# Moving both halves of the activations in one matmul, and adding the bank's halves afterwards

## The chip, the core and the metric

The kernel runs on one core of a Trainium2 chip. TensorE multiplies, with a queue of its own for the loads of its stationary operand (PEld in the profile); VectorE (DVE) and ScalarE (ACT) do everything that is not a matmul, GpSimd (POOL) almost nothing, and SyncE (SP) issues the DMAs. The metric is the device time of one launch in microseconds: 2150.61 before, the median of three runs (2150.57 to 2150.96).

## What is computed

256 tokens of width 2048 go through three layers, in fp32 from end to end, with matmul results that have to be close to true fp32:

```python
h  = mamba2(x)            # x @ a_w_in -> z, B, C, x (conv of 4 taps, silu), dt; chunked scan; @ a_w_out
x  = layernorm(ALPHA * x + h)
h  = window_attention(x)  # @ kv_w, @ b_w_in (queries and gates), softmax in a window, @ b_w_out
x  = layernorm(ALPHA * x + h)
x  = x + neighbourhood_attention(rms_norm(x))   # @ na_w_qkv_2, @ na_w_o_2
x  = x + (relu(rms_norm(x) @ mlp_w1_2) ** 2) @ mlp_w2_2
```

The batch is 1, so the weights are read once, for 256 tokens.

## The kernel before, in words

**Units.** The weights come as 357 units of 1 MB each, in one fixed order (`plan()`). A unit is loaded into one of three `raw` buffers, split by ACT into a high part `whi` (rounded to the matmul's narrower format, fp32r) and by DVE into the rest, `wlo = raw - whi`, and used by 24 or 48 matmuls. The activations stand split in the same way, as `A1h`, `A1l` (16 tiles of 128 features x 256 tokens each) or `A2h`, `A2l`. A product is three products: high x high, low x high, high x low.

**Two forms.** 232 units are of form "B" (`token_block`): the activations are stationary, the weights move 512 columns at a time, and a PSUM bank holds 128 tokens x 512 features. 125 units are of form "A" (`feature_block`): the weights are stationary, 128 x 128 for each of the 16 tiles of the contraction, and the activations of all 256 tokens move, so the result stands features by tokens in half a bank:

```python
e.matmul(o, wh, A1h[:, k, :], start=k == 0, stop=False)
e.matmul(o, wh, A1l[:, k, :], start=False, stop=False)
last = e.matmul(o, wl, A1h[:, k, :], start=False, stop=k == KT - 1)
```

That is 16 x 3 = 48 matmuls of 256 columns in an A unit. Lines 872, 873 and 874 are these three, lines 889, 890 and 891 the three of form B.

**Which units are A.** In each of the 8 groups of the Mamba layer `B`, `C` and four `x` units (48 in all, their results go through the 4-tap convolution) and one `dt` unit in the first; 16 units `g` of attention gates; 60 units `up` of the MLP, in four runs of 12 or 16, the 16 with nothing between them on TensorE.

**Emptying a bank.** There are four main banks, and an A unit takes one of them. `late(u)` empties unit u's bank while unit u + 1 is on TensorE. For the convolution ACT makes the first tap from PSUM (`Identity` with scale and bias, line 1180), DVE adds the three others from PSUM (line 1525), and ACT applies silu in `post(u)` (line 1207). For `g` ACT copies (line 1188), for `up` ACT applies relu (line 1197), DVE squares (line 1596), ACT rounds (line 1211) and DVE subtracts (line 1607).

**Order on the engines.** One list of steps (`script()`) is walked by every engine, and each issues its own part of each step, so every engine's order is fixed. At the start of unit u comes `late(u-1)`, then the splits of unit u + 2 (`hi`, line 1163 on ACT; `lo`, line 1563 on DVE, which waits for `hi`), then `post(u-1)`, the matmuls, the load of unit u + 5, and last the side work that a timetable puts behind the unit (the steps of the scan, `ssd(g, n)`; the attention's, `att(j, n)`). On TensorE side work is small matmuls and transposes in four other banks; among them are lines 951 and 953 (`heads_out`) of the scan, which wait for a product of DVE (line 1754) that waits for an exponential of ACT (line 1286).

Of the kernel before, what the change touches and what calls it, by code (L numbers as in the profile page):

```python
# [7 lines left out]
P = 128  # L8
D = 2048
T = 256  # L10
NT = T // P
KT = D // P
# [61 lines left out]

W_CUM, W_E = 0, 2048
W_XDT, W_XD, W_ZS, W_Y = 5120, 6144, 7168, 8192
W_CBM, W_XF, W_DTS = 9216, 9600, 11136
# [229 lines left out]
def stack_kernel(nc, wst, xT, xtok, pos, cols, rows, nabias, consts, out):  # L307
# [6 lines left out]
    with ExitStack() as ctx:  # L314
# [93 lines left out]
        conv_a = Marks(sem("conv_a"), *[words("id silu")] * 48)  # L408
        conv_v = Marks(sem("conv_v"), *[words("j1 j2")] * 48)
# [203 lines left out]
        PT = [W[:, N_PT + i * 512:N_PT + (i + 1) * 512] for i in range(2)]  # L613
        hb = [W[:, M_HB + t * 512:M_HB + (t + 1) * 512] for t in range(NT)]
        cs_t, sn_t = (SM[:, c:c + 32].rearrange("p (t h f) -> p t h f", t=NT, h=2) for c in (S_COS, S_SIN))
        dt_rows = [W[0:NH_S, W_E + i * T:W_E + (i + 1) * T] for i in range(11)]

        def xr(t, c):
# [214 lines left out]
        def tensor_program(e):  # L833
# [14 lines left out]
            def unit(u, t, ks):  # L848
                form, tag, *_ = units[u]
                o = bank[BANK[u, t]]  # L850
                if 0 in ks and BEFORE.get((u, t)):
                    w.wait_ge(*emptied(*BEFORE[u, t]))
                if form == "A":
                    feature_block(u, o[:, 0:T])
                else:
                    token_block(u, t, o[:, :], ks)

# [274 lines left out]
        def scalar_program(e):  # L1132
            w = Spare(e)

            def begin():
                for k in range(4):
                    w.wait_ge(s_x0[k], 16)
                    e.activation(A1h[:, k, :], W[:, k * T:(k + 1) * T], ACT.Copy).then_inc(*x_a.inc(f"h{k}"))
                    piece_hi(0, k)
                for c in (1, 2, 3):  # L1140
                    w.wait_ge(s_x[c], 16)
                    h = A1h[:, 4 * c:4 * c + 4, :].rearrange("p k t -> p (k t)")
                    e.activation(h, W[:, c * 1024:(c + 1) * 1024], ACT.Copy).then_inc(*x_a.inc(f"c{c}"))
                    if c < 3:
                        for k in range(4):
                            piece_hi(c, k)
# [22 lines left out]
            def late(u):  # L1169
                form, tag, *_ = units[u]  # L1170
                kind = tag[0]
                if kind in ("B", "C", "x"):
                    n, slot, c0 = conv_of(tag)
                    g = tag[1]
                    w.wait_ge(*mm((u, 0)))
                    if g:
                        w.wait_ge(*ssd_p("cb" if slot < 2 else "px", g - 1))
                    w.wait_ge(s_co, 16)
                    x_staged()
                    e.activation(xf[slot], bank[BANK[u, 0]][:, 0:T], ACT.Identity, scale=CO[:, c0 + 3:c0 + 4],  # L1180
                                 bias=CO[:, c0 + 4:c0 + 5]).then_inc(*conv_a.inc("id", n))
                elif kind == "g":
                    j, i = tag[1:]
                    w.wait_ge(*mm((u, 0)))
# [3 lines left out]
                    e.activation(gs[j % 2][:, i, :], bank[BANK[u, 0]][:, 0:T], ACT.Copy).then_inc(*evac_a.inc((u, 0)))  # L1188
                    if i == 3:
                        w.wait_ge(*evac_a((u, 0)))  # L1190
                        e.activation(gs[j % 2], gs[j % 2], ACT.Silu).then_inc(*gs_a.inc("s", j))
                elif kind == "up":
                    i = tag[2]
                    w.wait_ge(*mm((u, 0)))
                    if ups.index(u) >= 4:
                        w.wait_ge(*up_v("sq", ups[ups.index(u) - 4]))
                    e.activation(W[:, M_R + i % 4 * T:M_R + (i % 4 + 1) * T], bank[BANK[u, 0]][:, 0:T],  # L1197
                                 ACT.Relu).then_inc(*evac_a.inc((u, 0)))
                elif form == "B" and closes(tag):
                    evac(u, 1)  # L1200

            def post(u):
                tag = units[u][1]
                if tag[0] in ("B", "C", "x"):
                    n, slot, _ = conv_of(tag)
                    w.wait_ge(*evac_v((u, 0)))
                    e.activation(xf[slot], xf[slot], ACT.Silu).then_inc(*conv_a.inc("silu", n))
# [313 lines left out]
        def vector_program(e):  # L1521
# [5 lines left out]
            def begin():  # L1527
# [6 lines left out]
                                    ALU.subtract).then_inc(*x_v.inc(f"h{k}"))  # L1534
                    piece_lo(0, k)
                for c in (1, 2, 3):
                    h, low = (a[:, 4 * c:4 * c + 4, :].rearrange("p k t -> p (k t)") for a in (A1h, A1l))
                    w.wait_ge(s_x[c], 16)
                    w.wait_ge(*x_a(f"c{c}"))
                    e.tensor_tensor(low, W[:, c * 1024:(c + 1) * 1024], h, ALU.subtract).then_inc(*x_v.inc(f"c{c}"))  # L1540
                    if c < 3:
                        for k in range(4):
                            piece_lo(c, k)
# [22 lines left out]
            def late(u):  # L1566
                form, tag, *_ = units[u]
                kind = tag[0]
                ps = bank[BANK[u, 0]] if form == "A" else None
                if kind in ("B", "C", "x"):  # L1570
                    n, slot, c0 = conv_of(tag)
                    w.wait_ge(*mm((u, 0)))
                    w.wait_ge(*conv_a("id", n))
                    for j in (1, 2, 3):
                        if j > 1:
                            w.wait_ge(*conv_v(f"j{j - 1}", n))
                        k = mul_add(xf[slot][:, j:], ps[:, 0:T - j], CO[:, c0 + 3 - j:c0 + 4 - j], xf[slot][:, j:],
                                    ALU.mult, ALU.add)
                        k.then_inc(*(conv_v.inc(f"j{j}", n) if j < 3 else evac_v.inc((u, 0))))
                elif kind == "dt":  # L1580
                    z, v, *_ = dt_rows
                    w.wait_ge(*mm((u, 0)))
                    w.wait_ge(*x_a("c3"))
                    w.wait_ge(*x_v("c3"))
                    w.wait_ge(s_co, 16)
                    e.tensor_scalar(z, ps[0:NH_S, 0:T], CO[0:NH_S, C_DTB:C_DTB + 1], None,
                                    ALU.add).then_inc(*evac_v.inc((u, 0)))
                    w.wait_ge(*evac_v((u, 0)))
                    mul_add(v, z, -1.0, z, ALU.mult, ALU.max).then_inc(*dt_v.inc("abs"))
                elif kind == "up":  # L1590
                    i = tag[2]
                    r = W[:, M_R + i % 4 * T:M_R + (i % 4 + 1) * T]
                    w.wait_ge(*evac_a((u, 0)))
# [4 lines left out]
                elif form == "B" and closes(tag):  # L1598
                    evac(u, 1)

            def post(u):
                tag = units[u][1]
# [747 lines left out]
```

## Time and profile before

| | |
|---|---|
| median of three runs | 2150.61 us |
| the profiled execution | 2151.69 us, of which the span of instructions is 2149.9 us |
| TensorE busy | 2140.8 us, 100% of the span |
| its weight loads | 1887.3 us, 88% |
| VectorE busy | 1345.8 us, 63% |
| ScalarE busy | 1066.0 us, 50% |
| granted clock of TensorE | full in all 40 slices of the page |
| DMA | 399.92 MB, 186 GB/s on the mean |

The three columns of an instruction group in the profile are busy time, the mean duration of one, and the idle time of its engine before it. Matmuls overlap in the array, so the duration of one (285 ns for 256 columns) is longer than the distance from one start to the next. That distance is what a matmul costs in a stream, and it is read from starts and counts.

### The profile page before, as it was taken

What the parts mean: (1) busy time and instruction counts of PE and PEld (TensorE: products, weight loads), DVE (VectorE), ACT (ScalarE), POOL (GpSimd) and SP (SyncE); (2) the same over time, 40 slices, a digit from 0 to 9 for tenths busy, and PEclk for the clock granted to TensorE, in tenths of its full rate; (3) what the DMA queues carried; (4) which work ended last, traced back from release to release, by engine and by line L of the source; (5) the groups of instructions that cost most, each with busy time, mean ns of one, the idle gap of its engine ahead of it and who ended that gap; (6) DMA issues with size and microseconds to landing.
All of it is one profiled execution on the core that took longest, in us unless ns stands there. A gap on an engine that the chain in (4) does not pass through costs nothing.

```text
span 2149.9 us, 31131 instructions
## 1 busy us (share of the span) xinstructions
PE 2140.8 (100%) x12836; PEld 1887.3 (88%) x12836; DVE 1345.8 (63%) x1766; ACT 1066.0 (50%) x1315; POOL 39.8 (2%) x28
## 2 busy tenths in 40 slices
PE   9999999999999999999999999999999999999999
PEld 8989889889897888888888888889889989988987
DVE  7777767767768867665675566555545445545543
ACT  6766565464554555663555545544334433433432
POOL 0000000000000000000010011000000000000000
PEclk9999999999999999999999999999999999999999
DMA  8554555554544744445564554455554555555553
GB/s 311 211 197 177 193 185 181 187 195 177 191 181 157 231 161 146 154 157 196 190 214 169 189 189 157 157 196 179 194 196 177 190 191 188 180 194 195 178 205 127
DMA packets 62715, 399.92 MB, mean 186 GB/s; under 512 B 7088, under 2 KB 9840, under 8 KB 16112
## 3 DMA queue, kind: packets, MB, share of 16 engines
q1 hardware_dynamic: 62576, 397.95, 51.9%
q8 instruction: 102, 1.67, 0.3%
q14 instruction: 37, 0.30, 0.0%
HBM read 395.75 MB, written 2.16 MB: 185 GB/s over the span
## 4 chain that ended last, share of the span: by engine, by line
PE 98%; DVE 1%; DMA 0%; issue 0%; SPq 0%; ACT 0%; POOL 0%; DVEq 0%
PE bank L889 20%; PE bank L891 19%; PE bank L890 19%; PE bank L872 11%; PE bank L873 11%; PE bank L874 11%; PE bank L951 1%; PE bank L1099 1%; PE bank L1035 1%; PE bank L1057 0%; PE bank L994 0%; PE bank L1087 0%; PE bank L964 0%; DMA raw<-wst 0%; PE bank L1112 0%; PE bank L1068 0%
## 5 line engine op out<-in xcount | busy, mean ns | idle before, releaser
L1563 DVE TENSOR_TENSOR wlo<-raw,whi 128x2048 fp32r<-128x2048 f32 x353 | 808.4, 2291 | 493.8 <-ACT whi L1163 438.1
L1163 ACT ACTIVATE whi<-raw 128x2048 fp32r<-128x2048 f32 x353 | 674.6, 1911 | 455.7 <-PE bank L891 450.4
L872 PE MATMUL bank<-A1h,whi 128*128 128x256 f32 x2000 | 569.2, 285 | 0.0
L874 PE MATMUL bank<-A1h,wlo 128*128 128x256 f32 x2000 | 566.7, 283 | 0.0
L873 PE MATMUL bank<-A1l,whi 128*128 128x256 f32 x2000 | 566.7, 283 | 0.0
L889 PE MATMUL bank<-whi,A2h 128*128 128x512 f32 x1024 | 401.6, 392 | 0.0
L891 PE MATMUL bank<-wlo,A2h 128*128 128x512 f32 x1024 | 399.2, 390 | 0.0
L890 PE MATMUL bank<-whi,A2l 128*128 128x512 f32 x1024 | 399.0, 390 | 0.0
L872 PEld LDWEIGHTS bank<-A1h,whi 128*128 128x128 f32 x2000 | 384.2, 192 | 1.5 <-issue 1.2
L873 PEld LDWEIGHTS bank<-A1l,whi 128*128 128x128 f32 x2000 | 384.2, 192 | 0.3
L874 PEld LDWEIGHTS bank<-A1h,wlo 128*128 128x128 f32 x2000 | 384.1, 192 | 0.0
L889 PE MATMUL bank<-whi,A1h 128*128 128x512 f32 x832 | 330.7, 397 | 3.3 <-ACT whi L1153 2.5
L891 PE MATMUL bank<-wlo,A1h 128*128 128x512 f32 x832 | 324.6, 390 | 0.0
L890 PE MATMUL bank<-whi,A1l 128*128 128x512 f32 x832 | 324.5, 390 | 0.0
L891 PEld LDWEIGHTS bank<-wlo,A2h 128*128 128x128 f32 x1024 | 192.3, 188 | 40.3
L889 PEld LDWEIGHTS bank<-whi,A2h 128*128 128x128 f32 x1024 | 192.4, 188 | 39.3 <-issue 0.3
L890 PEld LDWEIGHTS bank<-whi,A2l 128*128 128x128 f32 x1024 | 192.5, 188 | 38.9
L889 PEld LDWEIGHTS bank<-whi,A1h 128*128 128x128 f32 x832 | 156.4, 188 | 38.7 <-issue 5.2
L891 PEld LDWEIGHTS bank<-wlo,A1h 128*128 128x128 f32 x832 | 156.2, 188 | 33.0
L890 PEld LDWEIGHTS bank<-whi,A1l 128*128 128x128 f32 x832 | 156.5, 188 | 30.2
L1197 ACT ACTIVATE W<-bank 128x256 f32<-128x256 f32 x60 | 23.0, 383 | 190.7 <-PE bank L874 190.7
L1525 DVE SCALAR_TENSOR_TENSOR W<-bank,CO,W 128x255 f32<-128x255 f32 x144 | 69.2, 481 | 51.4 <-ACT W L1180 48.0
(220 smaller groups left out, 1318.4 us busy)
## 6 DMA issues: line engine op xcount, KB each, us to landing
raw<-wst SPq DMA_DIRECT2D x353, 1024.0 KB, 4.8
W<-cum_scratch SPq DMA_DIRECT2D x8, 1024.0 KB, 6.9
W<-rows SPq DMA_DIRECT2D x21, 256.0 KB, 5.4
raw<-wst SPq DMA_DIRECT2D x16, 256.0 KB, 7.9
W<-nabias SPq DMA_DIRECT2D x16, 160.0 KB, 3.7
XR<-xtok SPq DMA_DIRECT2D x2, 1024.0 KB, 8.2
out<-XR SPq DMA_DIRECT2D x8, 256.0 KB, 2.3
W<-xT SPq DMA_DIRECT2D x3, 512.0 KB, 7.9
```

Of the source, the lines that this page charges most:

```text
L872: e.matmul(o, wh, A1h[:, k, :], start=k == 0, stop=False)
L873: e.matmul(o, wh, A1l[:, k, :], start=False, stop=False)
L874: last = e.matmul(o, wl, A1h[:, k, :], start=False, stop=k == KT - 1)
L889: e.matmul(o, h, wh, start=opens and k == 0, stop=False)
L890: e.matmul(o, low, wh, start=False, stop=False)
L891: last = e.matmul(o, h, wl, start=False, stop=closes(tag) and k == 3)
L951: e.matmul(o[c:c + 64, pr * T:(pr + 1) * T], x[0], E[:, h * 384:h * 384 + T], start=True, stop=False)
L1035: tr = e.transpose(o[:, i * P:(i + 1) * P], S8[:, h, i * P:(i + 1) * P], ident)
L1163: e.activation(whi[:, u % 3, :], raw[:, u % 3, :], ACT.Copy).then_inc(*hi.inc((u, 3)))
L1197: e.activation(W[:, M_R + i % 4 * T:M_R + (i % 4 + 1) * T], bank[BANK[u, 0]][:, 0:T], ACT.Relu).then_inc(*evac_a.inc((u, 0)))
L1525: return e.scalar_tensor_tensor(out=o, in0=a, scalar=s, in1=b, op0=op0, op1=op1)
L1563: e.tensor_tensor(wlo[:, u % 3, :], raw[:, u % 3, :], whi[:, u % 3, :], ALU.subtract).then_inc(*lo.inc((u, 3)))
```

## The change

`A1h` and `A1l` become the two halves of one tile `A1`, so that for each k the high and the low activations are 512 columns in a row. An A unit then takes a whole bank: `wh` moves both halves in one matmul of 512 columns, and `wl` moves the high half alone, into the bank's second half. The first half of the bank ends up with high x high, the second with low x high plus high x low. They are added when the bank is emptied: ACT copies the second half to SBUF, DVE adds the first half from PSUM to it, and the bank is free after the add. What ACT did before (scale and bias, relu) moves to DVE, behind the add. The core of the diff, first the tile and the matmuls:

```diff
-        A1h = sb("A1h", [P, KT, T], F32R)
-        A1l = sb("A1l", [P, KT, T], F32R)
+        A1 = sb("A1", [P, KT, 2, T], F32R)
+        A1h, A1l = A1[:, :, 0, :], A1[:, :, 1, :]
...
-        ON_ACT = ("z", "g", "nv", "nk", "nq", "upb", "up")
+        ON_ACT = ("z", "nv", "nk", "nq", "upb")
...
             def feature_block(u, o):
-                    e.matmul(o, wh, A1h[:, k, :], start=k == 0, stop=False)
-                    e.matmul(o, wh, A1l[:, k, :], start=False, stop=False)
-                    last = e.matmul(o, wl, A1h[:, k, :], start=False, stop=k == KT - 1)
+                    both = A1[:, k, :, :].rearrange("p h t -> p (h t)")
+                    if k < KT - 1:
+                        e.matmul(o[:, :], wh, both, start=k == 0, stop=False)
+                        e.matmul(o[:, T:2 * T], wl, A1h[:, k, :], start=False, stop=False)
+                    else:
+                        e.matmul(o[:, T:2 * T], wl, A1h[:, k, :], start=False, stop=False)
+                        last = e.matmul(o[:, :], wh, both, start=False, stop=True)
```

Emptying a unit of the convolution, on ScalarE (`rest` is the bank's second half; `g`, `up` and `dt` copy it likewise):

```diff
-                    e.activation(xf[slot], bank[BANK[u, 0]][:, 0:T], ACT.Identity, scale=CO[:, c0 + 3:c0 + 4],
-                                 bias=CO[:, c0 + 4:c0 + 5]).then_inc(*conv_a.inc("id", n))
+                    e.activation(xf[slot], rest, ACT.Copy).then_inc(*rest_a.inc(u))
```

The same on VectorE:

```diff
-                    w.wait_ge(*conv_a("id", n))
-                    for j in (1, 2, 3):
-                        k = mul_add(xf[slot][:, j:], ps[:, 0:T - j], CO[:, c0 + 3 - j:c0 + 4 - j], xf[slot][:, j:],
-                                    ALU.mult, ALU.add)
+                w.wait_ge(*rest_a(u))
+                    e.tensor_tensor(xu, ps, xf[slot], ALU.add).then_inc(*evac_v.inc((u, 0)))
+                    e.tensor_scalar(xf[slot], xu, CO[:, c0 + 3:c0 + 4], CO[:, c0 + 4:c0 + 5], ALU.mult,
+                                    ALU.add).then_inc(*conv_v.inc("j0", n))
+                    for j in (1, 2, 3):
+                        mul_add(xf[slot][:, j:], xu[:, 0:T - j], CO[:, c0 + 3 - j:c0 + 4 - j], xf[slot][:, j:],
+                                ALU.mult, ALU.add).then_inc(*conv_v.inc(f"j{j}", n))
```

On VectorE for the gates, then for the MLP:

```diff
+                    e.tensor_tensor(x, ps, x, ALU.add).then_inc(*evac_v.inc((u, 0)))
...
-                    e.tensor_tensor(W[:, M_H + i % 4 * T:M_H + (i % 4 + 1) * T], r, r,
-                                    ALU.mult).then_inc(*up_v.inc("sq", u))
+                    e.tensor_tensor(r, ps, r, ALU.add).then_inc(*evac_v.inc((u, 0)))
+                    mul_add(W[:, M_H + i % 4 * T:M_H + (i % 4 + 1) * T], r, 0.0, r, ALU.max,
+                            ALU.mult).then_inc(*up_v.inc("sq", u))
```

The silu over a gate's four units also moves, from `late` of the fourth to its `post`, behind the split of the next weights.

The order of TensorE's instructions at the end of the `dt` unit, the first A unit. Before, its last two tiles of the contraction:

```order
L872 MATMUL bank2<-A1h,whi 128x256
L873 MATMUL bank2<-A1l,whi 128x256
L874 MATMUL bank2<-A1h,wlo 128x256
L872 MATMUL bank2<-A1h,whi 128x256
L873 MATMUL bank2<-A1l,whi 128x256
L874 MATMUL bank2<-A1h,wlo 128x256
```

After:

```order
L877 MATMUL bank2<-A1,whi 128x512
L878 MATMUL bank2<-A1,wlo 128x256
L880 MATMUL bank2<-A1,wlo 128x256
L881 MATMUL bank2<-A1,whi 128x512
L896 MATMUL bank0<-whi,A1 128x512
```

Three matmuls of 256 columns for each tile have become one of 512 and one of 256; in the last tile the two stand in the other order, and a unit of form B follows.

VectorE, a unit of the convolution in group 0 (its bank is bank0), between two splits of weights. Before:

```order
L1525 SCALAR_TENSOR_TENSOR W<-bank0,CO,W 128x255
L1525 SCALAR_TENSOR_TENSOR W<-bank0,CO,W 128x254
L1525 SCALAR_TENSOR_TENSOR W<-bank0,CO,W 128x253
L1563 TENSOR_TENSOR wlo<-raw,whi 128x2048
```

After:

```order
L1609 TENSOR_TENSOR W<-bank0,W 128x256
L1612 TENSOR_SCALAR W<-W,CO 128x256
L1536 SCALAR_TENSOR_TENSOR W<-W,CO 128x255
L1536 SCALAR_TENSOR_TENSOR W<-W,CO 128x254
L1536 SCALAR_TENSOR_TENSOR W<-W,CO 128x253
L1575 TENSOR_TENSOR wlo<-raw,whi 128x2048
```

Two instructions more stand ahead of the split, and the three taps now read SBUF.

VectorE in a run of `up` units. Before:

```order
L1607 TENSOR_TENSOR A2l<-W,A2h 128x256
L1596 TENSOR_TENSOR W<-W 128x256
L1563 TENSOR_TENSOR wlo<-raw,whi 128x2048
```

After:

```order
L1625 TENSOR_TENSOR A2l<-W,A2h 128x256
L1599 TENSOR_TENSOR W<-bank2,W 128x256
L1536 SCALAR_TENSOR_TENSOR W<-W 128x256
L1575 TENSOR_TENSOR wlo<-raw,whi 128x2048
```

One instruction more, the add from the bank, and the square has become a max with zero times the value. SP's and POOL's orders are the same in both kernels.

## Rows read from the trace of the kernel before

**Rows 1.** The page: busy time, granted clock, and the chain that ended last.
```profile
PE 2140.8 (100%) x12836; PEld 1887.3 (88%) x12836; DVE 1345.8 (63%) x1766; ACT 1066.0 (50%) x1315; POOL 39.8 (2%) x28
...
PEclk9999999999999999999999999999999999999999
...
PE 98%; DVE 1%; DMA 0%; issue 0%; SPq 0%; ACT 0%; POOL 0%; DVEq 0%
```
**Rows 2.** Groups by line: count | busy us, mean ns | engine idle before, releaser.
```profile
L872 PE MATMUL bank<-A1h,whi 128*128 128x256 f32 x2000 | 569.2, 285 | 0.0
...
L872 PEld LDWEIGHTS bank<-A1h,whi 128*128 128x128 f32 x2000 | 384.2, 192 | 1.5 <-issue 1.2
```
**Rows 3.** Windows: us, then busy us (instructions) by engine, clock, DMA, GB/s.
```profile
1608.84:1700.99 92.15, 92.15 (x769) 92.14 (x768) 48.84 (x47) 39.26 (x46) 0.00 (x0) 1.00 0.52 183
1700.99:1788.06 87.07, 87.07 (x386) 72.13 (x385) 42.35 (x25) 31.23 (x18) 0.00 (x0) 1.00 0.53 193
```
**Rows 4.** Timeline of TensorE where 512 columns meet 256: start, us, instruction.
```profile
1608.62 0.39 PE L891 MATMUL bank<-wlo,A2h 128*128 128x512 f32 x1
1608.84 0.28 PE L872 MATMUL bank<-A1h,whi 128*128 128x256 f32 x1
...
1700.88 0.28 PE L874 MATMUL bank<-A1h,wlo 128*128 128x256 f32 x1
1700.99 0.40 PE L889 MATMUL bank<-whi,A2h 128*128 128x512 f32 x1
```
**Rows 5.** Groups by line and form: emptying banks and its nearest kin.
```profile
L1180 ACT ACTIVATE W<-bank,CO 128x256 f32<-128x256 f32 x48 | 27.0, 563 | 93.2 <-PE bank L874 93.2
L1525 DVE SCALAR_TENSOR_TENSOR W<-bank,CO,W 128x255 f32<-128x255 f32 x48 | 23.0, 480 | 48.0 <-ACT W L1180 48.0
L1197 ACT ACTIVATE W<-bank 128x256 f32<-128x256 f32 x60 | 23.0, 383 | 190.7 <-PE bank L874 190.7
L2168 DVE TENSOR_TENSOR A2l<-bank,A2h 128x256 fp32r<-128x256 f32 x16 | 6.7, 424 | 9.9 <-ACT A2h L1502 9.9
L2037 DVE TENSOR_SCALAR W<-W,SM 128x256 f32<-128x256 f32 x32 | 11.1, 348 | 0.0
```
**Rows 6.** Timeline of DVE in one convolution unit of group 4.
```profile
430.39 1.52 DVE L1525 SCALAR_TENSOR_TENSOR W<-bank,CO,W 128x255 f32<-128x255 f32 x3 [1.67 <-ACT W L1180]
432.19 2.29 DVE L1563 TENSOR_TENSOR wlo<-raw,whi 128x2048 fp32r<-128x2048 f32 x1 [0.28 <-ACT whi L1163]
```
**Rows 7.** Timeline of ACT and DVE in one `up` unit.
```profile
1620.56 0.38 ACT L1197 ACTIVATE W<-bank 128x256 f32<-128x256 f32 x1 [3.27 <-PE bank L874]
1620.97 0.43 DVE L1596 TENSOR_TENSOR W<-W 128x256 f32<-128x256 f32 x1 [1.27 <-ACT W L1197]
1622.83 2.29 DVE L1563 TENSOR_TENSOR wlo<-raw,whi 128x2048 fp32r<-128x2048 f32 x1 [1.43 <-ACT whi L1163]
```
**Rows 8.** Window: a convolution unit of group 0; columns as in rows 3.
```profile
42.80:48.50 5.70, 5.70 (x50) 5.70 (x49) 5.53 (x9) 2.79 (x3) 0.00 (x0) 1.00 0.61 207
```
**Rows 9.** Timeline: a split on DVE in group 0, and the start of its unit.
```profile
52.38 2.28 DVE L1563 TENSOR_TENSOR wlo<-raw,whi 128x2048 fp32r<-128x2048 f32 x1
...
60.63 0.37 PE L872 MATMUL bank<-A1h,whi 128*128 128x256 f32 x1
```
**Rows 10.** Timeline: the scan's chain beside an A unit, and who takes it up.
```profile
103.82 0.39 PE L953 MATMUL bank<-W 128*64 128x128 f32 x4
...
106.16 1.49 ACT L1286 ACTIVATE W<-W 128x1536 f32<-128x1536 f32 x1
...
107.68 1.76 DVE L1754 TENSOR_TENSOR W<-W 128x1536 f32<-128x1536 f32 x1 [4.13 <-ACT W L1286]
...
110.09 0.65 PE L951 MATMUL bank<-W 128*64 128x256 f32 x4
```
**Rows 11.** Timeline: the latest split of weights ahead of an A unit.
```profile
924.46 2.29 DVE L1563 TENSOR_TENSOR wlo<-raw,whi 128x2048 fp32r<-128x2048 f32 x1 [4.77 <-issue]
...
929.10 0.37 PE L872 MATMUL bank<-A1h,whi 128*128 128x256 f32 x1
```

More of the change, by code:

```diff
@@ L407, in stack_kernel @@
         set_v = Marks(sem("constants_set"), words("warm mh"))
-        conv_a = Marks(sem("conv_a"), *[words("id silu")] * 48)
-        conv_v = Marks(sem("conv_v"), *[words("j1 j2")] * 48)
+        rest_a = Marks(sem("second_half_out"), [u for u in range(NU) if units[u][0] == "A"])
+        conv_a = Marks(sem("conv_a"), *[words("silu")] * 48)
+        conv_v = Marks(sem("conv_v"), *[words("j0 j1 j2 j3")] * 48)
         dt_v = Marks(sem("dt_v"), words("abs s rec su s2 p0 c15 c13 c11 c9 c7 c5 c3 pf p2 dt dl dq dh dr ch cl dte copy"))
@@ L1171, in late @@
                 kind = tag[0]
[L1172 to L1177, printed above, removed]
+                if form == "B":
+                    if closes(tag):
+                        evac(u, 1)
+                    return
+                rest = bank[BANK[u, 0]][:, T:2 * T]
+                w.wait_ge(*mm((u, 0)))
+                if kind == "dt":
+                    x_staged()
                     w.wait_ge(s_co, 16)
-                    x_staged()
-                    e.activation(xf[slot], bank[BANK[u, 0]][:, 0:T], ACT.Identity, scale=CO[:, c0 + 3:c0 + 4],
-                                 bias=CO[:, c0 + 4:c0 + 5]).then_inc(*conv_a.inc("id", n))
+                    e.activation(dt_rows[0], rest[0:NH_S, :], ACT.Identity,
+                                 bias=CO[0:NH_S, C_DTB:C_DTB + 1]).then_inc(*rest_a.inc(u))
                 elif kind == "g":
                     j, i = tag[1:]
-                    w.wait_ge(*mm((u, 0)))
                     if j >= 2:
@@ L1187, in late @@
                         w.wait_ge(*gate_v((j - 2, 2, 1)))
[L1188 to L1191, printed above, removed]
+                    e.activation(gs[j % 2][:, i, :], rest, ACT.Copy).then_inc(*rest_a.inc(u))
                 elif kind == "up":
                     i = tag[2]
-                    w.wait_ge(*mm((u, 0)))
                     if ups.index(u) >= 4:
                         w.wait_ge(*up_v("sq", ups[ups.index(u) - 4]))
[L1197 to L1200, printed above, removed]
+                    e.activation(W[:, M_R + i % 4 * T:M_R + (i % 4 + 1) * T], rest, ACT.Copy).then_inc(*rest_a.inc(u))
+                else:
+                    n, slot, _ = conv_of(tag)
+                    g = tag[1]
+                    if g:
+                        w.wait_ge(*ssd_p("cb" if slot < 2 else "px", g - 1))
+                    x_staged()
+                    e.activation(xf[slot], rest, ACT.Copy).then_inc(*rest_a.inc(u))
             def post(u):
@@ L1205, in post @@
                     n, slot, _ = conv_of(tag)
+                    w.wait_ge(*conv_v("j3", n))
+                    e.activation(xf[slot], xf[slot], ACT.Silu).then_inc(*conv_a.inc("silu", n))
+                elif tag[0] == "g" and tag[2] == 3:
+                    j = tag[1]
                     w.wait_ge(*evac_v((u, 0)))
-                    e.activation(xf[slot], xf[slot], ACT.Silu).then_inc(*conv_a.inc("silu", n))
+                    e.activation(gs[j % 2], gs[j % 2], ACT.Silu).then_inc(*gs_a.inc("s", j))
                 elif tag[0] == "up":
@@ L1536, in begin @@
                 for c in (1, 2, 3):
[L1537 removed]
+                    h, low = (a[:, 4 * c:4 * c + 4, :] for a in (A1h, A1l))
+                    x = W[:, c * 1024:(c + 1) * 1024].rearrange("p (k t) -> p k t", k=4)
                     w.wait_ge(s_x[c], 16)
                     w.wait_ge(*x_a(f"c{c}"))
[L1540 removed]
+                    e.tensor_tensor(low, x, h, ALU.subtract).then_inc(*x_v.inc(f"c{c}"))
                     if c < 3:
@@ L1568, in late @@
                 kind = tag[0]
[L1569 to L1572, printed above, removed]
-                    w.wait_ge(*conv_a("id", n))
-                    for j in (1, 2, 3):
-                        if j > 1:
-                            w.wait_ge(*conv_v(f"j{j - 1}", n))
-                        k = mul_add(xf[slot][:, j:], ps[:, 0:T - j], CO[:, c0 + 3 - j:c0 + 4 - j], xf[slot][:, j:],
-                                    ALU.mult, ALU.add)
-                        k.then_inc(*(conv_v.inc(f"j{j}", n) if j < 3 else evac_v.inc((u, 0))))
-                elif kind == "dt":
-                    z, v, *_ = dt_rows
[L1582 to L1587, printed above, removed]
+                if form == "B":
+                    if closes(tag):
+                        evac(u, 1)
+                    return
+                ps = bank[BANK[u, 0]][:, 0:T]
+                w.wait_ge(*mm((u, 0)))
+                w.wait_ge(*rest_a(u))
+                if kind == "dt":
+                    z, v, *_ = dt_rows
+                    e.tensor_tensor(z, ps[0:NH_S, :], z, ALU.add).then_inc(*evac_v.inc((u, 0)))
                     w.wait_ge(*evac_v((u, 0)))
                     mul_add(v, z, -1.0, z, ALU.mult, ALU.max).then_inc(*dt_v.inc("abs"))
+                elif kind == "g":
+                    x = gs[tag[1] % 2][:, tag[2], :]
+                    e.tensor_tensor(x, ps, x, ALU.add).then_inc(*evac_v.inc((u, 0)))
                 elif kind == "up":
```

20 lines of the change are left out of this document (13 added, 7 removed).

## The prediction

> **What bounds the kernel now.** I read the page first. TensorE is busy in all of the span at the full clock, VectorE 63% and ScalarE 50% of it, and of the chain that ended last 98% is TensorE [rows 1]. So only what shortens TensorE's own stream, or makes it wait, can move the time; work on the other engines counts where it becomes late for TensorE.
>
> A busy TensorE says little of its pace, since matmuls overlap: one of 256 columns is recorded with 285 ns, and its weight load with 192 ns [rows 2]. The pace is read from starts and counts. The first window is a run of 16 `up` units with nothing between them: 16 x 48 = 768 matmuls of 256 columns (the 769th reaches in from before) in 92.15 us, or 119.99 ns each. The second is the run of 16 units of form B behind it: 384 matmuls of 512 columns in 87.07 us, or 226.74 ns each [rows 3]. The difference of the two, 106.75 ns, is what 256 more columns cost. Taken off either pace it leaves the same remainder: 119.99 - 106.75 = 13.24 ns, and 226.74 - 213.50 = 13.24 ns. It is paid once for each matmul with its load, however long the matmul is. The change moves as many columns as before (768 for each tile), in two matmuls in place of three.
>
> **The change part by part.**
>
> *Matmuls.* For each tile of an A unit: before 3 x 119.99 = 359.97 ns; after 226.74 + 119.99 = 346.73 ns; saved 13.24 ns. There are 2000 tiles (125 units of 16, the count of line 872 [rows 2]), so 26.5 us; a unit shrinks by 0.212 us, from 5.76 to 5.55. The trace has no stream in which 512 and 256 columns take turns, so the pair is bounded from both sides. Above, the pair could cost what three cost now, 360 ns, and nothing is gained. Below, the short matmul could cost its columns alone, 106.75 ns, for another 26.5 us; I exclude this, as the remainder stands whole at both lengths. I take the sum of the two paces because the trace shows both changes of length: from a 512 to the next start 0.22 us, and from a 256 to the start of a 512 0.11 us, each the ordinary distance of its own length [rows 4].
>
> The Trainium skill, "TensorE: Matmul & The Clock Gate", section "Back-to-back issue gap", gives N / 2.4 + 2.5 ns between starts at the warm clock, so a fixed part of only 2.5 ns. By it the three would cost 327.5 ns and the two 325.0 ns, the change would save 5.0 us, and the time would be 2145.6. The trace does not agree with it: 13.24 ns is left in both runs.
>
> *Emptying, ScalarE.* In the 48 convolution units a copy of 256 columns from PSUM (383 ns) takes the place of the scaled one (563 ns); in `up` and `g` a copy replaces an operation of its own size [rows 5]. ScalarE gets 8.6 us less, off the path.
>
> *Emptying, VectorE.* Each A unit gets an add with one side in PSUM; the nearest row has 424 ns. A convolution unit also gets a scale-and-bias in SBUF, 348 ns, while its three taps stay at 480 ns or a little under, now that they read SBUF [rows 5]. The square of `up` keeps its count. At most 48 x 0.77 + 76 x 0.42 = 69 us more on VectorE, 1415 of 2124 us, 67%. Is any of it in TensorE's way? By kind of unit:
>
> - Convolution, groups 1 to 7. The taps end at 431.91 and the split follows at 432.19, 0.28 us later, on ScalarE's account [rows 6]. The new chain starts 0.18 us earlier and is 0.77 us longer, so it ends at 432.50 and the split starts 0.3 us later. It is for the unit after next, which starts at about 441. Nothing.
> - Convolution, group 0, beside the small operations for `dt`. VectorE is busy 5.53 of 5.70 us there [rows 8], and the next three units look alike. With 0.77 more and a unit of 5.55 us it falls behind by some 0.75 us a unit, 3 us over four. The split of that stretch is done at 54.66 and its unit starts at 60.63, 5.97 us later [rows 9]. This cover holds, with about 3 us left; without it the rest would be a wait of TensorE, paid once.
> - `up`. VectorE's work ends at 1621.40 and it then waits 1.43 us for ScalarE's split [rows 7]. The add of 0.42 goes into this wait. The bank is free after about 1 us, and three more A units come before it is needed again.
> - `g`. Here too the add stands where VectorE waits for the split. The latest split ahead of an A unit is done at 926.75 and used at 929.10, 2.35 us later [rows 11]. It is far above the 0.21 us by which TensorE comes earlier.
> - The scan's chain. After line 953 ScalarE makes an exponential and VectorE a product that ends at 109.44, and TensorE takes it up at 110.09, behind an A unit: 0.65 us to spare [rows 10]. The unit between them shrinks by 0.21, which leaves 0.44. This is what is late next. ScalarE's silu now waits for a chain some 0.4 us longer, so the margin could go; I count 0.2 us for such small waits altogether.
>
> *Loads.* Weights are asked for at 1 MB in 5.55 us; form B's run already takes 1 MB in 5.44 us at a DMA share of 0.53 [rows 3]. No new bound.
>
> **Sum.** 26.5 - 0.2 = 26.3 us. The profiled execution took 2151.69 us, 1.79 outside the span, which gives 2125.4; the median of the runs is 1.08 lower, so **2124.3 us**.
>
> **The rivals.**
>
> 1. *The others' latency eats part of it.* In the `up` runs nothing but the splits stands beside TensorE, and their 60 x 0.212 = 12.7 us are safe. In the Mamba layer and the attention, 65 units, TensorE is followed closely by chains on the two other engines. If each took back what its unit saved, 13.8 us would go and the time would be 2138. For it: 0.65 us of margin [rows 10] and VectorE almost full in group 0 [rows 8]. Against it: the margins are several times 0.21 us elsewhere, and the chain of waits holds 1% of VectorE [rows 1]. Any time between 2129 and 2142 is this case: 0.06.
> 2. *The pair saves next to nothing,* because a short matmul between long ones costs more than in its own stream, or the fixed part is the 2.5 ns of the page named above: 2145 to 2151. Against it: the equal remainder [rows 3]. 0.04, half of it within 0.2%.
> 3. *Slower: the load of `wl` is no longer hidden.* Should the weight load of the short matmul begin only when the long one has left the array, the 192 ns of the load [rows 2] would stand in place of 120 ns: 72 ns more, 59 ns net of the saving, and 2000 pairs make 118 us, 2268 us. It decides from 13.24 ns a pair. Against it: in form B's run loads are hidden behind 512 columns, 72.13 us of loads in 87.07 with no loss [rows 3], and at a change of length too [rows 4]. 0.03.
>
> The forecast has 0.87, with a range of its own of 2122.5 to 2127: 13.24 ns is known to some tenths of a nanosecond (0.1 ns is 0.2 us), and small waits may cost up to 2 us or TensorE's present small waits shrink with the earlier start.
>
> **How the numbers follow.** The low end, 2121, is the forecast with 3 us more for a pair that is a little cheaper than the sum of its parts. The high end, 2130, takes in the first 6 us of rival 1. What is left out is the rest of rival 1, and rivals 2 and 3, together about 0.12. Faster by over 0.2% (4.3 us, about what a measurement of this kernel can tell from no change): the forecast, rival 1 and half of rival 2, 0.95. Within: the other half, 0.02. Slower: rival 3, 0.03.
>
> **What would show each step.** In the profile after, 16 `up` units of one run should take 16 x 16 x 0.34673 = 88.8 us in place of 92.15, and form B's run its 87.1 unchanged. TensorE should have 2000 matmuls and loads fewer and still be the whole chain. The split behind a convolution unit should start some 0.3 us later against its unit's start, with no idle time of TensorE released by VectorE or ScalarE. I am wrong if the pair in an `up` run is not 347 ns (then the matmul's cost was misread), or if it is and the Mamba layer shrinks by less than 10 us for its 49 units (then it is rival 1, and the group of waits names the chain).

## The result, and the profile after

The changed kernel takes **2137.63 us** (median of 4 runs, 2137.34 to 2138.11) where the kernel before took 2150.59 (4 runs, 2150.31 to 2150.96): a ratio of 0.994, 95% interval 0.9923 to 0.9957. It gains 13.0 us where 26.3 were forecast, and lies outside the range of 2121 to 2130. The profiled execution took 2137.87 us with a span of 2135.6.

The page of the changed kernel: the span, busy time by engine, the granted clock, the chain that ended last by engine, and groups of instructions (count | busy us, mean ns | idle before, releaser).

```profile
span 2135.6 us, 27302 instructions
...
PE 2126.5 (100%) x10836; PEld 1778.7 (83%) x10836; DVE 1413.4 (66%) x1938; ACT 1060.3 (50%) x1316; POOL 39.8 (2%) x28
...
PEclk9999999999999999999999999999999999999999
...
PE 94%; DVE 1%; ACT 0%; issue 0%; POOL 0%; DVEq 0%
...
L877 PE MATMUL bank<-A,whi 128*128 128x512 f32 x1875 | 668.8, 399 | 0.0
L878 PE MATMUL bank<-A,wlo 128*128 128x256 f32 x1875 | 526.4, 281 | 0.0
...
L1200 ACT ACTIVATE W<-bank 128x256 f32<-128x256 f32 x60 | 23.1, 386 | 184.5 <-PE bank L881 184.5
L1599 DVE TENSOR_TENSOR W<-bank,W 128x256 f32<-128x256 f32 x60 | 25.4, 424 | 72.4 <-ACT W L1200 72.4
```

TensorE has its 2000 matmuls and 2000 loads fewer and is 94% of the chain that ended last. That chain is TensorE's from 109.31 us on; before this it runs over VectorE and ScalarE, and it can be followed back only to 79.01 us (below, under the silus). The idle of lines 877 and 878 is 0.0, so within a unit there is no wait longer than what two matmuls overlap, and a loss there is one of pace (the emptying alone, below, has the same waits and no loss). The windows of the changed kernel over the same two stretches as in [rows 3] (a run of 16 `up` units, then form B's 16), and, third, the whole Mamba layer; columns as there:

```profile
1599.71:1690.16 90.45, 90.45 (x513) 78.43 (x512) 55.19 (x62) 39.28 (x46) 0.00 (x0) 1.00 0.52 186
1690.16:1777.21 87.05, 87.05 (x386) 72.08 (x384) 42.76 (x26) 31.23 (x18) 0.00 (x0) 1.00 0.54 193
...
25.07:688.14 663.07, 661.76 (x3519) 554.44 (x3517) 526.31 (x659) 376.67 (x449) 5.90 (x9) 1.00 0.54 194
```

Form B keeps its 87.05 us. The `up` run takes 90.45 us: 1.70 less than the 92.15 of before, and half of the 3.39 that were forecast (88.76). It holds 256 pairs, so a pair costs 353.3 ns and not 346.7, although VectorE, ScalarE and the loads leave nothing waiting. The timeline of TensorE inside one of its units shows where it goes:

```profile
1622.67 0.40 PE L877 MATMUL bank<-A,whi 128*128 128x512 f32 x1
1622.90 0.28 PE L878 MATMUL bank<-A,wlo 128*128 128x256 f32 x1
1623.02 0.40 PE L877 MATMUL bank<-A,whi 128*128 128x512 f32 x1
1623.26 0.28 PE L878 MATMUL bank<-A,wlo 128*128 128x256 f32 x1
1623.38 0.40 PE L877 MATMUL bank<-A,whi 128*128 128x512 f32 x1
1623.62 0.28 PE L878 MATMUL bank<-A,wlo 128*128 128x256 f32 x1
1623.73 0.40 PE L877 MATMUL bank<-A,whi 128*128 128x512 f32 x1
```

Three pairs take 1623.73 - 1622.67 = 1.06 us, 353 ns each. The next start comes 0.23 or 0.24 us behind a long matmul and 0.11 or 0.12 behind a short one. The trace's starts, to the nanosecond, repeat every three pairs (236 113 233 117 241 120):

```
233 113  233 117  241 120  236 113  233 117  241 120 ...   ns from one start to the next
```

So the long distances are 9.9 ns over the 226.74 of [rows 3] in the mean, and the short ones 3.3 ns under 119.99: 6.6 ns net a pair, or 106 ns a unit.

14 of the 125 units run otherwise. From their third pair on all of them hold a steady 230.0 and 116.6 ns, together 346.7: the forecast pair, although neither distance is that of its own run. This is one of them, in the Mamba layer of the same execution (three pairs in 1.04 us):

```profile
193.24 0.39 PE L877 MATMUL bank<-A,whi 128*128 128x512 f32 x1
193.47 0.28 PE L878 MATMUL bank<-A,wlo 128*128 128x256 f32 x1
193.58 0.39 PE L877 MATMUL bank<-A,whi 128*128 128x512 f32 x1
...
194.28 0.39 PE L877 MATMUL bank<-A,whi 128*128 128x512 f32 x1
```

**The account.** 111 units x 0.106 = 11.8 us. TensorE also waits twice at line 958 in the scan of group 0, 1.45 us in all (below). 26.5 - 11.8 - 1.45 = 13.3 us, and 13.0 were measured.

### The profile page after: what moved, and what is told of

Its sections match the earlier page's. It is cut to its first block, busy times and chain, and to the rows that moved or that the text cites. A ratio compares the mean times of both kernels' runs of the same rounds, so it can differ in the third digit from the quotient of the medians.

```text
span 2135.6 us, 27302 instructions
## 1 busy us (share of the span) xinstructions
PE 2126.5 (100%) x10836; PEld 1778.7 (83%) x10836; DVE 1413.4 (66%) x1938; ACT 1060.3 (50%) x1316; POOL 39.8 (2%) x28
## 4 chain that ended last, share of the span: by engine, by line
PE 94%; DVE 1%; ACT 0%; issue 0%; POOL 0%; DVEq 0%
PE bank L896 19%; PE bank L898 19%; PE bank L897 19%; PE bank L877 18%; PE bank L878 9%; PE bank L881 1%; PE bank L958 1%; PE bank L1106 1%; PE bank L880 1%; PE bank L1042 1%; PE bank L1064 0%; PE bank L1001 0%; PE bank L1094 0%; PE bank L971 0%; PE bank L1075 0%; PE bank L1119 0%
## 5 line engine op out<-in xcount | busy, mean ns | idle before, releaser
L877 PE MATMUL bank<-A,whi 128*128 128x512 f32 x1875 | 668.8, 399 | 0.0
L878 PE MATMUL bank<-A,wlo 128*128 128x256 f32 x1875 | 526.4, 281 | 0.0
L877 PEld LDWEIGHTS bank<-A,whi 128*128 128x128 f32 x1875 | 352.2, 188 | 81.8 <-issue 1.2
L878 PEld LDWEIGHTS bank<-A,wlo 128*128 128x128 f32 x1875 | 354.2, 189 | 4.5
L896 PE MATMUL bank<-whi,A 128*128 128x512 f32 x832 | 330.6, 397 | 2.2 <-ACT whi L1160 1.2
L898 PE MATMUL bank<-wlo,A 128*128 128x512 f32 x832 | 324.3, 390 | 0.0
L897 PE MATMUL bank<-whi,A 128*128 128x512 f32 x832 | 324.2, 390 | 0.0
L896 PEld LDWEIGHTS bank<-whi,A 128*128 128x128 f32 x832 | 156.3, 188 | 37.8 <-issue 5.8
L898 PEld LDWEIGHTS bank<-wlo,A 128*128 128x128 f32 x832 | 156.2, 188 | 33.2
L897 PEld LDWEIGHTS bank<-whi,A 128*128 128x128 f32 x832 | 156.6, 188 | 30.4
L1536 DVE SCALAR_TENSOR_TENSOR W<-W,CO 128x255 f32<-128x255 f32 x144 | 69.5, 483 | 5.1
L2210 POOL TENSOR_TENSOR SM<-SM 128x2 f32<-128x2 f32 (+2 forms) x24 | 39.6, 1654 | 1399.0 <-DVE SM L1789 649.2
```

The costliest lines, as they stand in the source:

```text
L877: e.matmul(o[:, :], wh, both, start=k == 0, stop=False)
L878: e.matmul(o[:, T:2 * T], wl, A1h[:, k, :], start=False, stop=False)
L896: e.matmul(o, h, wh, start=opens and k == 0, stop=False)
L897: e.matmul(o, low, wh, start=False, stop=False)
L898: last = e.matmul(o, h, wl, start=False, stop=closes(tag) and k == 3)
L1536: return e.scalar_tensor_tensor(out=o, in0=a, scalar=s, in1=b, op0=op0, op1=op1)
```

## The experiments

The theories, by the numbers that the expectations use: (1) a change of a matmul's length costs, whichever way the rest is arranged (1a: a fixed price for each change); (2) a long matmul of an A unit is dear whatever stands beside it; (3) the longer emptying makes TensorE wait, at line 958 above all; (4) the short matmul is dear, or makes the next one late, because it goes into the bank's second half; (5) it is the interleaved layout of the high and low activations. Each experiment leaves the rest of the changed kernel as it is; diffs are against it.

**Long ones first.** All 16 long matmuls of a unit, then its 16 short ones: the same work with one change of length each way.

```
-                    if k < KT - 1:
-                        e.matmul(o[:, :], wh, both, start=k == 0, stop=False)
-                        e.matmul(o[:, T:2 * T], wl, A1h[:, k, :], start=False, stop=False)
-                    else:
-                        e.matmul(o[:, T:2 * T], wl, A1h[:, k, :], start=False, stop=False)
-                        last = e.matmul(o[:, :], wh, both, start=False, stop=True)
+                    e.matmul(o[:, :], wh, both, start=k == 0, stop=False)
+                for k in range(KT):
+                    wl = wlo[:, s, k * P:(k + 1) * P]
+                    last = e.matmul(o[:, T:2 * T], wl, A1h[:, k, :], start=False, stop=k == KT - 1)
```

> The changed kernel, but each A unit issues its 16 matmuls of 512 columns first and then its 16 of 256, so the two lengths take turns once in a unit in place of 16 times. Theory 1 (taking turns costs it: in the changed kernel the pair takes 353.1 ns, 236.5 + 116.6, where 346.7 was forecast): the long ones return to 227 ns and the short ones to 120, an A unit takes 5.55 us in place of 5.65, and the time is 2137.6 - 12.7 = 2125 us. Theory 2 (512 moving columns of activations cost 236 ns whatever stands beside them, in this form of unit): the long ones stay at 236, the short ones go to 120, and the time is 2137 to 2144 us.

Measured: 2129.55 us (2128.91 to 2131.16) beside 2150.80, ratio 0.990 (0.9885 to 0.9915), 8.1 us under the changed kernel. Its `up` run, as a window:

```profile
1597.09:1686.13 89.04, 89.04 (x514) 78.72 (x512) 55.19 (x62) 39.26 (x46) 0.00 (x0) 1.00 0.54 189
```

A unit is 5.567 us, 20 ns over 16 x 346.7. Its distances show that the loss sits at the change and dies out behind it:

```
233 236 229 232 231 227 226 227 ... 226 | 114 119 120 120 ... 120
```

After the change to 512 five starts are late by 6, 9, 2, 5 and 4 ns, 26 together; after the change back two are early, 7 together. 26 - 7 is the 19 or 20 ns of a unit.

The 2125 us of theory 1 were missed by 4.6. The 20 ns that are left in a unit make 2.5 us over 125 units. The waits in front of the scan's matmuls (line 956 here) rose from 1.3 to 2.6 us of idle time. And in the profiled execution, itself 1.6 us above the median, TensorE waits for VectorE's split of the weights in group 0, which it does not do in the changed kernel:

```profile
65.65 3.91 PE L876 MATMUL bank<-A,whi 128*128 128x512 f32 x16 [1.18 <-DVE wlo L1573]
```

**Four products.** All matmuls long, so that the low weights meet the low activations too: a product that the reference's arithmetic leaves out, and 256 more columns a tile. There is no change of length at all inside a run. In place of the six lines that the first diff removes (so too in the next three):

```
+                    e.matmul(o[:, :], wh, both, start=k == 0, stop=False)
+                    last = e.matmul(o[:, :], wl, both, start=False, stop=k == KT - 1)
```

> The changed kernel with a fourth product: the low weights move both halves of the activations too (low x low is added to high x high), so that an A unit is 32 matmuls of 512 columns and nothing else. It computes one product more than before. Theory 1 (taking turns): 227 ns each, an up run of 16 units takes 16 x 32 x 0.2268 = 116.1 us. Theory 2 (512 columns of activations cost more): 236 ns each, 120.8 us.

Measured, in one run, 2338.73 us. The `up` run:

```profile
1723.76:1839.82 116.06, 116.06 (x514) 96.13 (x513) 55.19 (x62) 39.26 (x46) 0.00 (x0) 1.00 0.40 148
```

116.06 / 512 = 226.7 ns, form B's pace. The long matmul of an A unit is not dear by itself: theory 2 falls. Nor is it the taking turns of `whi` and `wlo` as the stationary operand, which is the same here.

**The emptying alone.** Three matmuls of 256 columns as before, the first into the bank's first half and the others into its second, and the emptying of the change.

```
+                    e.matmul(o[:, 0:T], wh, A1h[:, k, :], start=k == 0, stop=False)
+                    e.matmul(o[:, T:2 * T], wh, A1l[:, k, :], start=False, stop=False)
+                    last = e.matmul(o[:, T:2 * T], wl, A1h[:, k, :], start=False, stop=k == KT - 1)
```

> The emptying of the change without its matmuls: three matmuls of 256 columns for each tile as before, high x high into the bank's first half and the two others into its second; everything behind them as in the changed kernel. Theory 3 (the new work of ScalarE and VectorE makes TensorE wait in two places, in front of line 958 behind the first two tiles of the second scan group, 0.87 and 0.76 us by the profile): 2150.6 + 1 to 2 = 2152 us, with the waits in the same place and a little shorter, since an A unit is 0.11 us longer. If the new work costs more than these waits show: 2155 or more.

Measured: 2151.75 us (2150.87 to 2153.11, 10 runs), ratio 1.0005 (0.9995 to 1.0014). The `up` run:

```profile
1608.32:1700.47 92.15, 92.15 (x769) 92.15 (x768) 55.21 (x62) 39.25 (x46) 0.00 (x0) 1.00 0.51 183
```

It is the 92.15 us of [rows 3], with every distance at 120 ns. The longer emptying and the use of both halves are free in that run. Over the whole kernel the medians are 0.95 us apart, which the interval does not tell from nothing; TensorE waits 0.7 us at the line that is 958 in the changed kernel (954 here).

**In twos and in fours.** The same 32 matmuls a unit, with a change after every second, or every fourth, of a kind. For twos:

```
+                    e.matmul(o[:, :], wh, both, start=k == 0, stop=False)
+                    if k % 2:
+                        for j in (k - 1, k):
+                            last = e.matmul(o[:, T:2 * T], wlo[:, s, j * P:(j + 1) * P], A1h[:, j, :], start=False,
+                                            stop=j == KT - 1)
```

> The changed kernel with the matmuls of an A unit in the order 512, 512, 256, 256, so the lengths take turns half as often. Theory 1, if the cost is paid at each change of length: half of the 12.7 us comes back, 2131 us. If it is a rhythm that only strict alternation falls into: all of it, 2125 us. Theory 2 (512 columns of activations cost 236 ns anyway): none, 2137 us or more.

and for fours, with `k % 4 == 3` and `range(k - 3, k + 1)`:

> The changed kernel with an A unit's matmuls in the order four of 512, four of 256. The kernels so far give an up unit of 5.653 us (turns 16 times there and back), 5.573 (8 times) and 5.567 (once), against 5.547 for the plain sum of 16 x 346.7 ns. Theory 1a (a fixed cost for each change of length): between 8 times and once, 5.57 us a unit. Theory 1b (after a change to 512 columns the next five matmuls start late, by 6, 9, 2, 5 and 4 ns, and after one to 256 the next two early, by 6 and 1; a shorter run cuts this off): 4 x (233 + 236 + 229 + 232 + 114 + 119 + 120 + 120) = 5.612 us a unit, slower than in twos, and about 2134.5 us.

Measured, one run each: 2131.34 us in twos, 2134.02 in fours. The `up` run in twos:

```profile
1597.38:1686.54 89.16, 89.16 (x513) 77.80 (x512) 55.20 (x62) 39.25 (x46) 0.00 (x0) 1.00 0.52 189
```

and in fours:

```profile
1597.79:1687.58 89.79, 89.79 (x514) 78.48 (x512) 55.20 (x62) 39.28 (x46) 0.00 (x0) 1.00 0.53 188
```

Their distances, one period each:

```
twos   233 231  113 119   233 236  116 113
fours  235 234 236 224  117 120 120 120   234 235 229 232  118 119 117 117
```

| changes in a unit | form | unit, us | over 16 x 346.7 ns |
|---|---|---|---|
| 2 | sixteens | 5.567 | 20 ns |
| 8 | fours | 5.613 | 66 ns |
| 16 | twos | 5.573 | 26 ns |
| 30 | the change | 5.653 | 106 ns |

No fixed price for a change fits: 8 changes cost more than 16. In fours the 16 distances above sum to 2807 ns where 8 x 346.73 is 2774, two such periods a unit make the 66 ns. The unit is the 5.61 us that replaying the sixteens' distances gave, but the single distances are others (235 234 236 224 where 233 236 229 232 were replayed), and in twos the same replay gives 8 x (233 + 236 + 114 + 119) = 5.616 us where 5.573 were measured. So its hit in fours is no proof of it. Nor is the total of the twos one for the toll: 2131.34 us is the 2131 that half of the loss would give, but their `up` run gets back 1.29 of the 1.69 us that the changed kernel's loses, and waits of TensorE in group 0 hide the rest (2.5 us at the scan's matmuls, 0.8 for a split). What is shown is that the loss comes with taking turns and that its size depends on the rhythm; it is not a toll (theory 1a), and no rule tried here gives the size for every rhythm.

**The first half.** The short matmul writes the bank's first half, where the following long one begins, in place of the second.

```
-                        e.matmul(o[:, T:2 * T], wl, A1h[:, k, :], start=False, stop=False)
+                        e.matmul(o[:, 0:T], wl, A1h[:, k, :], start=False, stop=False)
```

> The changed kernel, but the short matmul adds into the bank's first half (high x high) and not its second. Theory 1 (the lengths alone): the same as the changed kernel, an up run of 16 units in 90.45 us and 2137.6 us. Theory 4 (the short matmul adds where the long one has just written, and the next long one follows on the same words): the distances change, an up run differs by more than 0.3 us.

**The tiles apart.** The high and low activations in two blocks, as before the change; the long matmul reads one tile of each.

```
-        A1 = sb("A1", [P, KT, 2, T], F32R)
-        A1h, A1l = A1[:, :, 0, :], A1[:, :, 1, :]
+        A1 = sb("A1", [P, 2, KT, T], F32R)
+        A1h, A1l = A1[:, 0, :, :], A1[:, 1, :, :]
...
-                    both = A1[:, k, :, :].rearrange("p h t -> p (h t)")
+                    both = A1[:, :, k, :]
...
```

> The changed kernel, but with the high and the low activations 16 KB apart in a partition as two rows that one matmul reads after each other, not as 512 neighbouring columns. Theory 1 (the lengths alone): the same as the changed kernel, 90.45 us for an up run and 2137.6 us. Theory 5 (where the moving columns stand in SBUF, against the loads of the weights): an up run differs by more than 0.3 us, and the layout of the change is part of its cost or of its gain.

Measured, one run each: 2139.00 us with the first half, 2137.72 with the tiles apart. The `up` run with the first half:

```profile
1600.82:1691.26 90.44, 90.44 (x513) 78.48 (x512) 55.19 (x62) 39.25 (x46) 0.00 (x0) 1.00 0.52 186
```

and with the tiles apart:

```profile
1599.64:1690.09 90.45, 90.45 (x513) 78.48 (x512) 55.19 (x62) 39.24 (x46) 0.00 (x0) 1.00 0.53 186
```

Both keep the 90.45 us of the changed kernel to 0.01. Theories 4 and 5 fall. Of the 1.4 us that the first one is longer as a whole, 0.9 are a longer wait at line 958, 2.2 us where the changed kernel has 1.3; with the tiles apart it is 0.7.

**The silus behind the exponential.** That wait is the other loss. The changed kernel's groups of waits (waited for: us in total, times, longest), and its timeline in the scan of group 0:

```profile
PE bank L958 <- DVE W L1772: 1.3, 2, 0.7
...
ACT W L1214 <- DVE W L1536: 56.6, 47, 5.3
```

```profile
94.90 0.42 ACT L1214 ACTIVATE W<-W 128x256 f32<-128x256 f32 x1 [1.86 <-DVE W L1536]
...
98.02 1.49 ACT L1297 ACTIVATE W<-W 128x1536 f32<-128x1536 f32 x1
...
99.54 1.76 DVE L1772 TENSOR_TENSOR W<-W 128x1536 f32<-128x1536 f32 x1 [2.47 <-ACT W L1297]
...
100.25 0.39 PE L881 MATMUL bank<-A,whi 128*128 128x512 f32 x1
...
101.35 0.65 PE L958 MATMUL bank<-W 128*64 128x256 f32 x4 [0.71 <-DVE W L1772]
```

Read upwards: TensorE's line 958 follows 1.10 us behind line 881, where 0.32 is usual (so it is behind a long matmul in all other groups), and 0.78 us are lost. It waits for the product of line 1772, this for the exponential of line 1297, and this stands on ScalarE's queue behind the silu of line 1214, which waits 1.86 us for the taps. At 109.31 the same happens for 0.67 us. (The idle time of the profile, 0.71 and 0.60, counts from the modelled end of line 881.) In all, silus wait 56.6 us for the taps; in the kernel before it was 9.4 us, 11 times. With the long matmuls first it is worse: there the two waits are 1.95 and 0.67 us.

The chain that ended last says where the lateness comes from (start, us, what):

```profile
79.01 1.95 issue
80.96 0.43 DVE W L1609
...
96.72 1.28 ACT L1297
98.02 1.50 ACT W L1297
```

Between 57.90 and 79.02 VectorE is busy 20.52 of 21.12 us, and from there the two engines hand the work to each other without a pause for TensorE. So this chain did not move forward when TensorE became faster. In the kernel before, the first product was ready at 99.93 and TensorE took it up at 102.69, 2.76 us later; now it is ready at 101.30, and TensorE would have come at 100.57.

The experiment takes the version with the long matmuls first and lets the silus of `x` 0 and `x` 1 of group 1 follow the exponential on ScalarE. No wait is taken away by hand; two instructions, which stand in `conv_silu` now, are issued later.

```
             def post(u):
...
-                    n, slot, _ = conv_of(tag)
-                    w.wait_ge(*conv_v("j3", n))
-                    e.activation(xf[slot], xf[slot], ACT.Silu).then_inc(*conv_a.inc("silu", n))
+                    if tag not in (("x", 1, 0), ("x", 1, 1)):
+                        conv_silu(tag)
...
+                if g == 0 and n in (9, 10):
+                    conv_silu(("x", 1, n - 9))
```

> The kernel with the long matmuls first, and on ScalarE the silu of two convolution units of the second group (x 0 and x 1) behind the exponential of the scan's chain instead of ahead of it. Theory 3 (the wait of TensorE in front of the scan's matmuls, 2.9 us together in the kernel with the long ones first, comes from this silu, which now waits for VectorE's longer chain while the exponential stands behind it): both waits go, 2129.6 - 2.7 = 2127 us. If the chain is late for another reason (VectorE's queue alone), the waits stay and the time is 2129 to 2130.

Measured: **2127.55 us** (2126.98 to 2128.13) beside 2150.84, ratio 0.9892 (0.9875 to 0.9908), 2.0 us under the version with the old order of silus. Its timeline at the same place:

```profile
95.48 1.49 ACT L1301 ACTIVATE W<-W 128x1536 f32<-128x1536 f32 x1
...
97.00 1.76 DVE L1776 TENSOR_TENSOR W<-W 128x1536 f32<-128x1536 f32 x1 [0.19 <-ACT W L1301]
...
98.28 0.42 ACT L1210 ACTIVATE W<-W 128x256 f32<-128x256 f32 x1
...
100.16 0.65 PE L956 MATMUL bank<-W 128*64 128x256 f32 x4
```

The product ends at 98.76, 1.4 us ahead of its use, and line 956 waits for nothing. A comparison inside the traces bears this out without the totals: from the first add (line 1609 in the changed kernel, at 59.43 us) behind the two scan instructions of group 0 to the first exponential it is 38.59 or 38.60 us in the changed kernel, the emptying alone, long ones first, twos, fours, first half and tiles apart, and 36.30 us here. The 2.29 us are the silu's wait of 1.86 and the silu itself, 0.42. What differs between the other seven is when this chain starts (58.88 to 60.90 us) and when TensorE comes, and so the wait of 0.7 to 2.6 us; why it starts when it does stays open. The version with the silus moved is the fastest of the study, and it comes within 3.3 us of the forecast for the change as it was made.

## Why the prediction was wrong

**What bounds the kernel, and the two paces: right.** TensorE is still the bound; 226.7 ns for a run of 512 and 120 for a run of 256 were found again (form B 87.05 us, four products 116.06, the emptying alone 92.15). The long-first version gained 21 us, so the fixed part of 13.24 ns is real and paid back per matmul removed. The 2.5 ns of the Trainium skill, "TensorE: Matmul & The Clock Gate", "Back-to-back issue gap", would leave 5 us to gain, so the runs do not agree with them. The section gives them for an isolated matmul and says that in a stream the weight loads count too, which the prediction left out.

**The step that failed: "I take the sum of the two paces because the trace shows both changes of length: from a 512 to the next start 0.22 us, and from a 256 to the start of a 512 0.11 us".** Each is the distance behind the last matmul of the old length, where nothing is to be seen yet. The price stands in the starts that follow. The trace of before held it, right behind the last row of [rows 4], in its timeline of TensorE:

```profile
1701.23 0.40 PE L890 MATMUL bank<-whi,A2l 128*128 128x512 f32 x1
1701.46 0.39 PE L891 MATMUL bank<-wlo,A2h 128*128 128x512 f32 x1
1701.69 0.40 PE L889 MATMUL bank<-whi,A2h 128*128 128x512 f32 x1
1701.92 0.39 PE L890 MATMUL bank<-whi,A2l 128*128 128x512 f32 x1
1702.16 0.39 PE L891 MATMUL bank<-wlo,A2h 128*128 128x512 f32 x1
1702.38 0.39 PE L889 MATMUL bank<-whi,A2h 128*128 128x512 f32 x1
```

From 1700.99 five distances take 1.17 us, where 5 x 0.22674 is 1.13; to the nanosecond they are 233, 236, 228, 232 and 232, within 1 ns those of the long-first version. Then it is 226 or 227. Even this could not have given 353.3: sixteens, fours and twos show that the sum depends on the rhythm. But it would have said that a pair in strict alternation, which never has five equal neighbours, was not bounded by the two runs. The bound that the prediction named above, 360 ns, was the place to widen the range to; rival 2 (a pair that saves next to nothing) came near the mechanism in its first clause, at half the price, though it is the long matmuls that are dear and the short ones early. Of 26.5 us this step is off by 11.8.

**The band that the time fell into is not its cause.** The prediction gave 2129 to 2142 us to rival 1, with 2138 as its sum, and 2137.63 were measured. That is chance. Rival 1 held the 12.7 us of the `up` units safe, and they gave about 6.4 (60 x 0.106); its own mechanism, the waits for other engines, cost 1.45 us.

**Emptying on ScalarE and VectorE: nearly right.** ScalarE has 5.7 us less (8.6 forecast); VectorE has 1413.4 us (at most 1415). The add is 424 ns as its kin, the scale-and-bias 413 ns where 348 was taken, the taps 483 as before. In a unit of group 4 the way from ScalarE's copy to the end of the taps is 2.91 us (420.56 to 423.47) where it was 2.18, so 0.73 longer and not 0.59. In groups 1 to 7, `up` and `g` it costs TensorE nothing, as forecast: 92.15 us for the emptying alone.

**The scan's chain: right place, wrong size.** "This is what is late next" holds; the 0.2 us counted for small waits were 1.45. The step took the 0.65 us of [rows 10] as the margin and took 0.21 off it, for one unit. But the chain is not started by TensorE: it hangs on VectorE's queue from group 0 on, so the 2.76 us in front of the first product went as well: TensorE comes 2.12 us earlier there, by all that it gained up to that point, and the chain is 1.37 us later. The prediction did name the silu's longer wait, with 0.4 us, and did not follow it into the exponential behind it. That is rival 1, and it is shown by the silus' move, which shortens the chain by 2.29 us and takes the wait away.

**Convolution, group 0: the wrong unit.** "This cover holds, with about 3 us left" is right for the unit that was read (3.14 us). The next one is the tight one. Its split and its start, before and then in the changed kernel:

```profile
59.29 2.28 DVE L1563 TENSOR_TENSOR wlo<-raw,whi 128x2048 fp32r<-128x2048 f32 x1
66.46 0.28 PE L872 MATMUL bank<-A1h,whi 128*128 128x256 f32 x1
...
61.74 2.28 DVE L1575 TENSOR_TENSOR wlo<-raw,whi 128x2048 fp32r<-128x2048 f32 x1
65.06 0.40 PE L877 MATMUL bank<-A,whi 128*128 128x512 f32 x1
```

From the end of the split to the start of the unit there were 4.89 us, and 1.04 are left. The faster orders use them up: TensorE waited there 1.18 us in the profile of the long ones first and 0.75 in twos.

**The test that the prediction set itself** ("wrong if the pair in an `up` run is not 347 ns") decided at once: 353.3. The Mamba layer shrinks by 5.0 us (668.06 to 663.07) where 49 x 0.212 = 10.4 were due: 37 of its units without the steady rhythm cost 3.9, the waits 1.45. Rival 3, the exposed load, is excluded: it would put 192 ns in place of 120 in every pair, and in the `up` run no start comes later than 121 ns behind a short matmul or 241 behind a long one.

**What stays open.** Why a matmul that follows another length starts late or early, and what sets a unit into the steady 230.0 and 116.6. The steady ones recur in place (`x` 3 of groups 0 and 2 to 7, `B` of groups 3 to 7, two of `g`), so it looks like a matter of how a unit begins, but no run here tells what. The five versions that ran once (four products, twos, fours, first half, tiles apart) are read by their `up` runs, not by their totals.

## What to carry to other kernels

Two lengths of matmul, each priced in a run of its own, may not be added up for a stream in which they take turns: look at the five or six starts behind a change of length, and if the order is free, put like lengths together. Where a unit's emptying becomes longer on one engine, look on the other engine for an in-order instruction that waits for it, and at what is queued behind that one; the margin is not that of the last link alone. And where that chain runs on by itself, take off its margin all that the faster engine has gained by then.

## What the runs showed of the hardware that was not expected

- After a change from 256 to 512 columns five starts come late (26 ns together), after the reverse two come early (7 ns). In strict alternation the starts settle into a period of three pairs, at 353.3 ns for a pair, or in 14 of 125 units into a steady 346.7, which is the sum of the two paces.
- More changes can cost less: 16 in a unit 26 ns, 8 in a unit 66 ns.
- Which half of a bank a short matmul writes, and whether a 512-column operand lies in one block or in two, makes no difference to the pace (90.44 and 90.45 us).
